# Bias of layer two from two products on six partitions, and four transpositions of layer one placed later

## What is computed

```python
lv = lam_vecs.astype(jnp.float32)
lam = jnp.exp(jnp.sum(lv[0] * lv[1])) - jnp.exp(jnp.sum(lv[2] * lv[3])) + lam_init
table = rel_bias.astype(jnp.float32)          # 32 buckets x 6 heads
...
logits = jnp.einsum('bhmqd,bhmkd->bhmqk', qb, k).astype(jnp.float32)
bias = table[t5_bucket(key_pos[None, :] - q_pos[:, None])]
logits = logits + jnp.transpose(bias, (2, 0, 1))[None, :, None]
```

## Time and profile before

| | us |
|---|---|
| median of 3 runs | 1934.56 |
| lowest and highest | 1932.63, 1938.84 |
| profiled execution | 1933.61 |
| its span, first to last instruction | 1931.8 |
| mean granted TensorE clock | 0.966 |

### The profile page before, as it was taken

The page is one execution under the profiler, slowest core; times in us unless marked ns, Lnnn a source line. Parts: engine busy times, 40 slices in busy tenths (PEclk is TensorE's granted clock), DMA queues, the critical chain, the costliest instruction groups (busy, mean ns, idle before and its releaser), DMA issues.

```text
span 1931.8 us, 28399 instructions
## 1 busy us (share of the span) xinstructions
PE 1803.0 (93%) x11800; PEld 1444.1 (75%) x11800; DVE 955.4 (49%) x1645; ACT 542.9 (28%) x1090; POOL 704.1 (36%) x333
## 2 busy tenths in 40 slices
PE   8999888889788988986999999999999899999999
PEld 5688667777676676764888888887777588888887
DVE  6675256566644434555566654123345266555411
ACT  3111112344423154545322221003422332222100
POOL 4333100000243311321655555454323275555542
PEclk9999999998898899998999999998999899999999
DMA  5222210000131411210322233331112133332222
GB/s 175 66 87 94 65 45 3 3 2 2 35 122 63 136 36 58 68 53 22 97 93 97 97 99 98 98 99 60 55 57 67 41 100 98 99 97 95 94 96 77
DMA packets 43205, 142.48 MB, mean 74 GB/s; under 512 B 5267, under 2 KB 7077, under 8 KB 42950
## 3 DMA queue, kind: packets, MB, share of 16 engines
q1 hardware_dynamic: 43078, 140.67, 22.3%
HBM read 136.06 MB, written 4.06 MB: 73 GB/s over the span
## 4 chain that ended last, share of the span: by engine, by line
PE 50%; DVE 2%; ACT 2%; issue 1%; POOL 1%; DMA 0%; DVEq 0%; SPq 0%; ACTq 0%
PE b_p_bank L206 16%; PE b_p_bank L208 15%; PE b_p_bank L207 15%; PE b_p_bank L2559 0%; PE b_p_bank L2554 0%; POOL b_wlo L187 0%; PE b_p_bank L2541 0%; DVE l_sc L2183 0%; PE b_p_bank L1890 0%; DVE l_mx L2189 0%; PE b_p_bank L1866 0%; PE b_p_bank L2498 0%; PE b_p_bank L2497 0%; DVE l3t_ke L2672 0%; DMA gate_w<-in_gate_w 0%
## 5 line engine op out<-in xcount | busy, mean ns | idle before, releaser
L187 POOL TENSOR_TENSOR b_wlo<-b_raw,b_whi 128x1024 fp32r<-128x1024 f32 x238 | 582.6, 2451 | 830.7 <-DVE b_whi L180 830.7
L206 PE MATMUL b_p_bank<-b_hi,b_whi 128*128 128x512 f32 x1008 | 407.4, 404 | 7.6 <-PEq L71 6.6
L180 DVE CAST b_whi<-b_raw 128x1024 fp32r<-128x1024 f32 x238 | 182.2, 773 | 457.6 <-PE b_p_bank L208 388.0
L208 PE MATMUL b_p_bank<-b_hi,b_wlo 128*128 128x512 f32 x1008 | 397.1, 394 | 0.0
L207 PE MATMUL b_p_bank<-b_lo,b_whi 128*128 128x512 f32 x1008 | 397.1, 394 | 0.0
L206 PEld LDWEIGHTS b_p_bank<-b_hi,b_whi 128*128 128x128 f32 x1008 | 192.0, 191 | 52.9 <-issue 13.4
L207 PEld LDWEIGHTS b_p_bank<-b_lo,b_whi 128*128 128x128 f32 x1008 | 192.1, 191 | 40.8 <-issue 2.6
L208 PEld LDWEIGHTS b_p_bank<-b_hi,b_wlo 128*128 128x128 f32 x1008 | 191.9, 190 | 41.0
L206 PE MATMUL b_p_bank<-f_mhi,b_whi 128*128 128x512 f32 x352 | 136.9, 389 | 0.0
L207 PE MATMUL b_p_bank<-f_mlo,b_whi 128*128 128x512 f32 x352 | 136.9, 389 | 0.0
L208 PE MATMUL b_p_bank<-f_mhi,b_wlo 128*128 128x512 f32 x352 | 136.9, 389 | 0.0
(11 more groups left out here) (428 smaller groups left out, 3106.4 us busy)
## 6 DMA issues: line engine op xcount, KB each, us to landing
b_raw<-in_w_up SPq DMA_DIRECT2D x88, 512.0 KB, 3.6
b_raw<-in_w_down SPq DMA_DIRECT2D x44, 512.0 KB, 3.6
b_raw<-in_w_in SPq DMA_DIRECT2D x32, 512.0 KB, 3.6
b_raw<-in_w_out SPq DMA_DIRECT2D x24, 512.0 KB, 3.6
b_raw<-in_w_gla SPq DMA_DIRECT2D x22, 512.0 KB, 3.7
b_raw<-in_w_diff SPq DMA_DIRECT2D x20, 512.0 KB, 3.7
b_raw<-in_w_mem SPq DMA_DIRECT2D x8, 512.0 KB, 3.7
all_x<-in_x SPq DMA_DIRECT2D x8, 256.0 KB, 6.0
```

The lines of the kernel that those rows point to most:

```text
L180: self.nc.vector.tensor_copy(self.hi[:, n % SLOTS, :], self.raw[:, n % RAWS, :]).then_inc(self.s_hi, 1)
L187: self.nc.gpsimd.tensor_tensor(self.lo[:, n % SLOTS, :], self.raw[:, n % RAWS, :], self.hi[:, n % SLOTS, :].bitcast(F32), ALU.subtract).th ...
L206: nc.tensor.matmul(acc, lhsT=left[0], rhs=right[0], start=first, stop=False)
L208: return nc.tensor.matmul(acc, lhsT=left[1], rhs=right[0], start=False, stop=last)
```

## The change

`Bias` multiplies the 32x6 table itself with the buckets, in two products (512 and 128 columns) whose result has the six heads' lines on partitions 0 to 5. `spread` and its copy are gone, and ten of twelve products. VectorE makes two copies of 6 partitions into `row`, now 6x640. SyncE issues six stores, one behind the other; each reads one partition's line 128 times. There is a semaphore for each head's store. The part has 4 steps instead of 9, lambda's product comes in the second, and the first three strips are loaded in the fourth. The plan of that stretch keeps 24 portions and is written anew. In layer one `early` is 26: turns 4 to 7 are mixed into the compression.

```diff
-    early = len(order)
+    early = len(order) - 4
...
-    n = DH + 3
+    n = 4
...
-        self.row, self.lv = shelf.sb("row", [P, 2, REL]), shelf.sb("lv", [1, 2, 2, HD])
-        self.spread = shelf.sb("spread", [RB, DH, P])
+        self.row, self.lv = shelf.sb("row", [DH, REL]), shelf.sb("lv", [1, 2, 2, HD])
...
     def put(self, sp, h):
-        sp.wait_ge(self.s_row, 2 * h + 2)
-        sp.dma_start(self.line[h, :, :], self.row[:, h % 2, :]).then_inc(self.s_line[h % 2], 16)
+        src = self.row[h:h + 1, :].unsqueeze(1).broadcast_to([1, P, REL])
+        sp.dma_start(self.line[h:h + 1, :, :], src).then_inc(self.s_line[h], 16)
...
     def sync(self, sp):
         yield
-        for h in range(DH + 2):
-            if h >= 1 and h - 1 < DH:
-                self.put(sp, h - 1)
-            if 3 <= h < 6:
-                self.fetch(sp, h - 3)
-            yield
+        sp.wait_ge(self.s_row, 2)
+        for h in range(DH):
+            self.put(sp, h)
+        yield
+        yield
+        for h in range(3):
+            self.fetch(sp, h)
+        yield
...
-        for h in range(DH):
-            for n, (a, b) in enumerate(self.parts):
-                if h >= 1:
-                    pe.wait_ge(self.s_row, 2 * h - 1 + n)
-                self.nc.tensor.matmul(self.ps[n][:, 0:b - a], lhsT=self.spread[:, h, :], rhs=self.bucket[:, a:b],
-                                      start=True, stop=True).then_inc(self.s_b, 1)
-            yield
+        for n, (a, b) in enumerate(self.parts):
+            self.nc.tensor.matmul(self.ps[n][0:DH, 0:b - a], lhsT=self.table[:, :], rhs=self.bucket[:, a:b],
+                                  start=True, stop=True).then_inc(self.s_b, 1)
+        yield
...
-        for h in range(DH):
-            for n, (a, b) in enumerate(self.parts):
-                dve.wait_ge(self.s_b, 2 * h + n + 1)
-                if h >= 2:
-                    dve.wait_ge(self.s_line[h % 2], 16 * (h // 2))
-                nc.vector.tensor_copy(self.row[:, h % 2, a:b], self.ps[n][:, 0:b - a]).then_inc(self.s_row, 1)
-            yield
+        yield
+        for n, (a, b) in enumerate(self.parts):
+            dve.wait_ge(self.s_b, n + 1)
+            nc.vector.tensor_copy(self.row[:, a:b], self.ps[n][0:DH, 0:b - a]).then_inc(self.s_row, 1)
         yield
...
-                for i in range(2):
-                    dve.wait_ge(self.bias.s_line[i], 16 * (DH // 2))
+                for i in range(DH):
+                    dve.wait_ge(self.bias.s_line[i], 16)
...
-    plan += spread(4, 13) + spread(18, 15) + [0, 1, 0, 1, 0]
+    plan += [0, 1, 0, 1, 0, 1] + spread(6, 5) + spread(13, 15) + [0, 1, 0, 1, 0]
```

More of the change, by code:

```diff
@@ L1656, in __init__ @@
         self.ps, self.pl, self.banks_free = banks, small, banks_free
-        (self.i_t, self.i_b, self.i_l, self.s_b, self.s_row, l0, l1, self.s_d, self.s_pl, self.s_e, self.s_end,
-         self.s_sp) = sems(nc, tag, "it", "ib", "il", "b", "row", "line0", "line1", "d", "pl", "e", "end", "spread")
-        self.s_line = [l0, l1]
+        (self.i_t, self.i_b, self.i_l, self.s_b, self.s_row, self.s_d, self.s_pl, self.s_e, self.s_end) = sems(
+            nc, tag, "it", "ib", "il", "b", "row", "d", "pl", "e", "end")
+        self.s_line = sems(nc, tag, *(f"line{h}" for h in range(DH)))
         self.s_strip = sems(nc, tag, *(f"strip{h}" for h in range(DH)))
@@ L1669, in put @@
     def put(self, sp, h):
-        sp.wait_ge(self.s_row, 2 * h + 2)
-        sp.dma_start(self.line[h, :, :], self.row[:, h % 2, :]).then_inc(self.s_line[h % 2], 16)
+        src = self.row[h:h + 1, :].unsqueeze(1).broadcast_to([1, P, REL])
+        sp.dma_start(self.line[h:h + 1, :, :], src).then_inc(self.s_line[h], 16)
     def fetch(self, sp, h):
-        sp.wait_ge(self.s_line[h % 2], 16 * (h // 2) + 16)
+        sp.wait_ge(self.s_line[h], 16)
         src = bass.AP(tensor=self.line.tensor, offset=h * P * REL + P - 1, ap=[[REL - 1, P], [1, T]])
@@ L1680, in sync @@
         yield
-        for h in range(DH + 2):
-            if h >= 1 and h - 1 < DH:
-                self.put(sp, h - 1)
-            if 3 <= h < 6:
-                self.fetch(sp, h - 3)
-            yield
+        sp.wait_ge(self.s_row, 2)
[6 more added lines that the diff above has]
+        yield
     def tensor(self, pe):
+        pe.wait_ge(self.i_t, 16)
         pe.wait_ge(self.i_b, 16)
-        pe.wait_ge(self.s_sp, 1)
         pe.wait_ge(*self.banks_free)
-        for h in range(DH):
-            for n, (a, b) in enumerate(self.parts):
-                if h >= 1:
-                    pe.wait_ge(self.s_row, 2 * h - 1 + n)
-                self.nc.tensor.matmul(self.ps[n][:, 0:b - a], lhsT=self.spread[:, h, :], rhs=self.bucket[:, a:b],
-                                      start=True, stop=True).then_inc(self.s_b, 1)
-            yield
+        for n, (a, b) in enumerate(self.parts):
+            self.nc.tensor.matmul(self.ps[n][0:DH, 0:b - a], lhsT=self.table[:, :], rhs=self.bucket[:, a:b],
+                                  start=True, stop=True).then_inc(self.s_b, 1)
+        yield
         pe.wait_ge(self.s_d, 2)
@@ L1705, in vector @@
         nc, lv, lam = self.nc, self.lv, self.lam
-        dve.wait_ge(self.i_t, 16)
-        nc.vector.tensor_copy(self.spread[:, :, :], self.table[:, :].unsqueeze(2).broadcast_to([RB, DH, P])
-                              ).then_inc(self.s_sp, 1)
         dve.wait_ge(self.i_l, 16)
```

## The result

| | before | after |
|---|---|---|
| median, us | 1934.32 (4 runs) | 1958.31 (4 runs) |
| lowest and highest | 1932.63, 1938.84 | 1953.07, 1963.11 |
| profiled execution | 1933.61 | 1953.79 |

The change makes the kernel slower, by a ratio of 1.012 (interval 1.0081 to 1.0159). The forecast of 1915.3 us has the wrong sign and the median lies outside its range; the rival "one row, one path" is what happened. The four executions stand in two pairs, 1953.07 and 1953.79, 1962.83 and 1963.11 us. The profiled one is of the faster pair; where the other pair loses 9 us more is not shown here.

The account below looks back on a forecast made before the run. TensorE, busy 93% of the span, was taken to bound the kernel. Second-layer stages (16.7 + 2.7 + 0.5 - 1.5 = 18.4) plus 0.9 in the first layer gave 19.3 us less, 1915.3 us; range 1909 to 1956.

Parts of the forecast that it names:

- one row, one path: Rival: reads of one partition's row pass one after the other, six stores take 88 us, VectorE's cast waits, 1968 us; chance 0.26.
- The six stores: Bias stores, each reading one partition 128 times: all issued within 2 us near 654, together taking 7 to 14 us.
- My own 88 us: Upper bound for the six bias stores: 14.6 us each if one row's reads pass serially at a DMA engine's 20 to 22 GB/s.
- The deadline: Weight tile queued behind the stores, needed at VectorE's cast near 691 us: up to some 31 us of stores costs nothing.
- The sum: Whole kernel: 18.4 us gained in the second layer plus 0.9 in the first, 19.3 us in all.
- Stage one: Second layer, first bias product to the keys' first sum, 22.26 us before: 16.7 us gained.
- Stage two: Second layer, keys' first sum to step 1 of memory attention, 11.1 us, now covering 4 portions of projection: 2.7 us gained.
- Stage three: Second layer, steps 1 to 4 of memory attention, 11.1 us before: 0.5 us gained, bounds 0 and 2.4.
- Stage four: Second layer, steps 4 to 13 of memory attention, 11 portions before, 8 now: 1.5 us lost, between 0.8 and 2.2.
- step 13 "near 708": Sign that the forecast is right: step 13 of memory attention in the second layer comes near 708 us.
- The clock rival: TensorE stays at 1.2 GHz between the keys' sums and in memory attention's first steps, first layer loses: 6 to 9 us; 0.11.
- First layer: Turns 4 to 7 moved from projection's end to compression: 5.2 us gained there, net 0.9 gained; bounds 2.5 gained, 1.5 lost.

Follow-up runs that it names:

- e_two_far: Changed kernel, each head's row in partitions h and h + 64, both read by its store; one execution 1935.5 us, first bias product to difference attention's first exponential 81.7 us.
- e_two_near: Changed kernel, each head's row in partitions h and h + 32, both read by its store; one execution 1964.9 us, first bias product to difference attention's first exponential 120.0 us.

## Why the prediction was wrong, point by point

**The six stores.** This is the step that failed: "I take the lower end, since the number and size of pieces and their target are those of the old store". The source was what counted: at the measured 27 GB/s the six took 72.8 us, 12.1 us a store, between the prediction's bounds of 7 to 14 and 88 us, and the cast waited 32.8 us. That "all six are issued within 2 us" failed with it: the six issues took 47 us (6.1 us with rows in 16 partitions). The prediction named the point from which it decides (53 us) and the consequence, and gave it 0.26. The one sentence with a figure for a single path came from the Trainium skill, "SBUF — State Buffer", section "Door 1: The DMA port swizzle", by whose rule the six would take 72 us and the time would be 1952; the trace agrees with the 72. That the profiled execution took 1953.8 is in part luck, and the median was 1958.3: the stretch came out 23.2 us longer than before, and 2.9 us came back behind it. My own 88 us came from the rate of one busy DMA engine (20 to 22 GB/s) and missed the measured 27 by a fifth.

**The deadline.** "Up to some 31 us" was close: stores of 36 us (`e_two_far`) made VectorE wait 2.4 us, and the time of the stores less the wait is 34, 40 and 38 us in the three kernels with a stall. The cast was the one that I named, reached at 695.3, where I had 691.

**The sum.** With the stores out of the way the kernel is 10.4 us faster by the ratio where 19.3 were forecast, so the sum was too high as well. By stages, in the 16-partition kernel: **Stage one**, 16.7 us forecast: 14.8 (22.26 before, 10.21 now, less two portions of 1.36). The ten products and the waits for copies went as forecast; mis-sized was the clock, which I took to stay up and which is 0.73 from 660 to 665 us, behind the bias products. **Stage two**, 2.7 us: 11.14 us for 11.1 forecast, right, with the waits of 1.4 and 1.9 us (1.6 and 2.2 forecast). **Stage three**, 0.5 us gained: it was 1.2 us lost. I had bounded it at 0 from below; the wait in front of step 1, 1.9 us where it had been 0.43, is followed by the lower clock. **Stage four**, 1.5 us lost: 3.5 by the same count, since the bare step 7 saved nothing and cost the step behind it. Together 12.8 instead of 18.4 us. The sign of step 13 "near 708" didn't follow from these stages, which put it at 710. The clock rival was the right mechanism in the main, and a case of its own with only 0.11: it had 6 to 9 us of the sum go, and with the first layer 6.7 went. It had the clock wrong between the keys' sums, where it stayed at 1.00.

**First layer**, 0.9 us gained: 0.2 us lost by the keys' product. The gain in the projection was 5.5 (5.2 forecast), the loss behind it 5.7 (4.3). ScalarE's sigmoid did stand behind the copies of turns 4 and 5; the first hidden product came 3.8 us later against the projection's end, not 2.2. This term was mis-sized on both sides and nearly cancels.

## What to carry to other kernels

Before a row is sent out of one partition instead of 128, ask from how many of the shared paths (ports) the transfer reads, and divide its bytes by their rate, some 25 GB/s each here; then look which load stands behind it in the same queue and which engine will stand in line for it. Sixteen copies of a row cost TensorE nothing here (10.2 us from the first product to the keys' first sum with 6 rows and with 96); they need one copy of the product's left operand on VectorE, 1.8 us, and bring the store from some 12 us down to 4.7. Work that is freed in one place should be put where an engine still waits and where the clock falls: with the same 24 portions the stretch got 12.8 or 20.9 us shorter by their places alone.

## What the hardware showed that I had not expected

A path out of the on-chip memory gives 23 to 28 GB/s whether a store reads one, two or four of its partitions, and partitions 0 to 3 and 32 share one. While it is the bound, the busy share of the DMA engines says nothing of the load: it was 0.9 at 27 GB/s with six stores queued from one partition each, and 0.12 at 25 to 27 GB/s with six queued from two partitions of one path (`e_two_near`, 690 to 720 us). And slow stores hold SyncE itself at the issue in both (six issues in 47 and 51 us, the load behind them 11.4 and 12.0), so they delay even the issue of what follows.
